# Second mixer of a two-block kernel: index heads and top-k among the projections, late attention heads in pairs, one chunk's weight residue on GpSimd

## The chip, the cores and the metric

One NeuronCore of a Trainium2 chip. The metric is the device time of one execution of the whole kernel in microseconds (us). A core has five engines that run their own instruction lists in order and wait for each other on semaphores: TensorE (PE, matmuls into PSUM; PEld is its weight load), VectorE (DVE), ScalarE (ACT), GpSimd (POOL) and SyncE (SP, which issues DMAs here).

## The reference, cut to what matters

Two blocks run one after the other on 256 tokens of width 1024. The first (three attention branches) and the expert layer at the end are untouched. Between them stands the second block's mixer:

```python
h = rms_norm_2(x, norm1_g) * (1 + scale1) + shift1
proj = h @ w_in                       # 3656 columns
xc, bg, cg, q, k, v, qi, ki, wi = jnp.split(proj, cuts, axis=-1)
conv_out = bg * short_conv(cg * xc, conv_w)
q = apply_partial_rope(rms_norm_2(q.reshape(B, S, 8, 64), q_norm_g), positions)
k = apply_partial_rope(rms_norm_2(k.reshape(B, S, 8, 64), k_norm_g), positions)
qi = apply_partial_rope(qi.reshape(B, S, 8, 64), positions)
ki = apply_partial_rope(rms_norm_2(ki, kidx_norm_g), positions)
# dsa_attention: an index picks the 64 keys that each query sees
rel = relu(einsum('bqhd,bsd->bqhs', qi, ki))
score = einsum('bqhs,bqh->bqs', rel, wi) * IDX_SCALE     # causal, then top_k
s = einsum('bqhd,bqkhd->bhqk', q, k_selected) * 64 ** -0.5
o = einsum('bhqk,bqkhd->bqhd', softmax(s), v_selected)
mix = concatenate([conv_out, attn_out], axis=-1) @ w_out
x = x + gate1 * mix                   # then norm, router, 64 experts (top 8)
```

So q, k, v and the softmax need the selection only at the scores, and the index needs only qi, ki and wi.

## The kernel before, in words

Tokens lie on partitions in NT = 2 tiles of 128. One list, `SCHEDULE` (`make_schedule`, L151 to L225), gives the order of all steps up to the router. Every engine walks this same list and issues its own part of each step, so the order of the list is the order on each engine.

**Projections.** `proj2` takes the input columns in eight chunks (`CHUNKS2`, L73): 0 qi, 1 kiwi (ki and wi, 72 columns), 2 q2, 3 k2, 4 v2, 5 xc, 6 cg, 7 bg; each for t = 0, 1 (called the first and the second half of a chunk below). A weight chunk (2 MB, 8.0 us to land) comes into one of two ring slots by SP (L533); a slot is free when the chunk two back is fully split. fp32 products are made from two parts: ScalarE rounds the chunk to an upper half `w_hi` (L787, four pieces), VectorE subtracts it from the original to get the lower half `w_lo` (L1045, four pieces), and TensorE multiplies a_hi w_hi, a_lo w_hi and a_hi w_lo: 24 matmuls a half (L1585), or 48 of half width for the three convolution chunks xc, cg, bg (L1582). There is one pair of `w_hi`, `w_lo` buffers: a piece of the next chunk may be rounded once TensorE has used the same piece in the second half (`w_used`). `with_splits` (L117) therefore puts the four `split` steps of the next chunk between the second half's matmuls and its `drain`, the step in which ScalarE or VectorE empties the PSUM bank. Two PSUM banks (`proj_b`) alternate; `bank_free` of a half lets the half after next start.

**Drains.** qi: a copy (L1111). q2, k2, kiwi: square on ScalarE (L804), sum on VectorE (L1079), power on GpSimd (L644, L648), then scaling and gains on VectorE (L1100, L1106), whose last instruction frees the bank. v2, xc: a copy on ScalarE (L810). cg: a product into `uT` (L1130). bg: three-tap convolution and product (L1143 to L1151), about 3.7 us for one half.

**Rest of the mixer.** `angles` (L1295) makes rope's arguments on VectorE, ScalarE takes the sine (L871), `rope` (L1318) rotates 25 rows of heads (q 0 to 7, k 8 to 15, qi 16 to 23, ki 24, copied to 25). `turn2` transposes the rows to T2 (L1640, copied out by ScalarE at L866) through one PSUM bank, in four groups g (q, k, qi, ki) of two tiles. `index` (L1679, relu L877, weighted sum L1333) and `topk` (L1346, a chain of MAX8 and MATCH_REPLACE) give `selmask`. For each head n = 24 to 31: `score` (two matmuls, L1677), logits plus mask (L1242), maximum (L1257), exp (L887), `flip` (transposes L1700, copied by L898), `value` (L1724), scaling by 1/sum into O2 (L1282). The logits have two buffers. Before head i's `value` matmul TensorE waits until all earlier heads have been scaled:

```python
                    if i >= 1:

                        pe.wait_ge(S("valued"), 2 * i)
```

The order around it (L205 to L221): qi, kiwi, `angles`, q2, k2, `rope`, v2, `turn2`, eight `index`, `topk` 0, xc first half, `topk` 1, xc second half; then heads 24 to 31 by `head` (L176), which puts one conv half (cg, cg, bg, bg) into each of the first four heads and none into the last four. In head n it also places `value` n-2 before that half's drain on every engine, and `flip` n-1 after it. Last the convolution rows and the turned O2 are split (`mix_conv`, `turn_branch` 3) and `out2` multiplies them.

Of the kernel before, what the change touches and what calls it, by code (L numbers as in the profile page):

```python
# [93 lines left out]
FILL2 = [1, 1, 1, 1, 0, 0, 0, 0]  # L94
# [56 lines left out]
def make_schedule():  # L151
# [53 lines left out]
    for c in range(4):  # L205
        s.extend(("proj2", c, t) for t in range(NT))
        if c == 1:
            s.append(("angles",))
    s.append(("rope",))
    groups = [[("proj2", c, t)] for c in range(4, 8) for t in range(NT)]  # L210
    take(2)
    s.append(("turn2",))
    s.extend(("index", h) for h in range(8))
    s.append(("topk", 0))
    take(1)
    s.append(("topk", 1))
# [58 lines left out]

TURNS = []
for _it in SCHEDULE:
    if _it[0] == "turn":
        TURNS.append(_it)
    if _it[0] == "turn_branch":  # L280
        TURNS += [_it + (t,) for t in range(NT)]
    if _it[0] in ("turn_merged", "norm", "start"):
        TURNS += [_it + (t, q) for t in range(NT) for q in range(2)]
    if _it[0] == "ada_out":
        TURNS.append(_it)
    if _it[0] == "turn2":
        TURNS += [_it + (g, t) for g in range(4) for t in range(NT)]
# [18 lines left out]
def build(nc, a, out):  # L306
    ctx = ExitStack()
    with ctx:
# [31 lines left out]
        nmax = sb("neg_max", [P, 2, 2])  # L340
        den = sb("den", [P, 2, 2])
        rden = sb("rden", [P, 2, 2])
# [293 lines left out]
        def _(gp):  # L636
# [15 lines left out]
            for it in RESULTS:  # L652
# [83 lines left out]
        def _(act):  # L736
# [19 lines left out]
            for it in RESULTS:  # L756
# [104 lines left out]
                if it[0] == "turn2":  # L861
                    for g in range(4):
# [15 lines left out]
                if it[0] == "score_rest":  # L878
# [5 lines left out]
                    for t in range(NT):  # L884
                        lo, w = (0, P + sink) if t == 0 else (P + 1, 2 * P + sink)
                        v = L[:, i % 2, 0:ng, lo:lo + w]
                        act.activation(v, v, ACT.Exp, bias=nmax[:, i % 2, t:t + 1],  # L887
                                       accum_out=den[:, i % 2, t:t + 1]).then_inc(S("probs"), 1)
# [73 lines left out]
        def _(dve):  # L962
# [14 lines left out]
            for it in RESULTS:  # L977
# [62 lines left out]
                if kind0 == "split":  # L1040
# [180 lines left out]
                if kind0 in ("score", "score_rest"):  # L1221
# [4 lines left out]
                    buf = L[:, i % 2]  # L1226
# [18 lines left out]
                if kind0 == "score_rest":  # L1245
# [9 lines left out]
                    for t in range(NT):  # L1255
                        lo, w = (0, P + sink) if t == 0 else (P + 1, 2 * P + sink)
                        dve.tensor_reduce(nmax[:, i % 2, t:t + 1], buf[:, 0:ng, lo:lo + w],  # L1257
                                          AX.XY, ALU.max, negate=True).then_inc(S("maxed"), 1)
                if kind0 == "flip":
# [4 lines left out]
                    dve.reciprocal(rden[:, i % 2, :], den[:, i % 2, :]).then_inc(S("rden_ready"), 1)  # L1264
                if kind0 == "value":
# [3 lines left out]
                    for t in range(NT):  # L1269
                        dve.wait_ge(S("value_product"), 2 * i + 2)  # L1270
                        ps = value_b[:, 128 * (i % 2) + 64 * t:128 * (i % 2) + 64 * t + 64]
                        if n < 24:
# [5 lines left out]
                            dve.scalar_tensor_tensor(out=o, in0=ps, scalar=rden[:, i % 2, t:t + 1], in1=o,  # L1278
                                                     op0=ALU.mult, op1=ALU.mult).then_inc(S("valued"), 1)
                        else:  # L1280
                            o = O2[:, t, HD * (n - 24):HD * (n - 24) + HD]
                            dve.tensor_scalar(o, ps, rden[:, i % 2, t:t + 1], None, ALU.mult).then_inc(S("valued"), 1)  # L1282
                if kind0 in ("angles", "rope"):
                    step = S(kind0 + "_step")
                    k = 0
# [32 lines left out]
                if kind0 == "rope":  # L1318
                    dve.wait_ge(S("trig_ready"), 1)

                    bank_taken(dve, USE["proj2", 3, 1])
                    for t in range(NT):
                        lo, hi = R[:, t, 0:25, 0:8], R[:, t, 0:25, 8:16]
                        cos = trig[:, t, 0:1, :].to_broadcast([P, 25, 8])
                        sin = trig[:, t, 1:2, :].to_broadcast([P, 25, 8])
                        for b, (src, f) in enumerate(((lo, cos), (hi, sin), (hi, cos), (lo, sin))):
                            chain(dve.tensor_tensor(rt[:, b], src, f, ALU.mult))
                        chain(dve.tensor_tensor(lo, rt[:, 0], rt[:, 1], ALU.subtract))
                        chain(dve.tensor_tensor(hi, rt[:, 2], rt[:, 3], ALU.add))
                        dve.tensor_copy(R[:, t, 25, :], R[:, t, 24, :]).then_inc(S("rows_ready"), 1)  # L1330
# [183 lines left out]
        def _(pe):  # L1514
# [18 lines left out]
            for it in SCHEDULE:  # L1533
# [99 lines left out]
                if kind0 == "turn2":  # L1633
                    pe.wait_ge(S("rows_ready"), NT)
                    for g in range(4):
# [20 lines left out]
                if kind0 in ("score", "score_rest"):  # L1656
                    n = it[1]
                    ng = len(units_of(n)) if n < 24 else 1
                    for g in range(0 if kind0 == "score" else 2, min(2, ng) if kind0 == "score" else ng):
# [10 lines left out]
                        else:  # L1670
# [20 lines left out]
                if kind0 == "flip":  # L1691
                    n = it[1]
                    i = HEADS.index(n)
                    for g in range(len(units_of(n)) if n < 24 else 1):
# [4 lines left out]
                        for b, lo in enumerate((0, P + 1, 2 * P + 1)):  # L1699
                            mm = pe.transpose(flip_b[u % 2][:, b * P:(b + 1) * P], L[:, i % 2, g, lo:lo + P], ident)  # L1700
# [240 lines left out]
```

## Time and profile before

| | |
|---|---|
| time, median of 3 runs (lowest, highest) | 1218.96 us (1215.31, 1219.78) |
| the profiled execution: own time, span in the trace | 1215.82 us, 1214.0 us |
| PE busy, share of span | 1066.8 us, 88% |
| DVE busy | 800.2 us, 66% |
| ACT busy | 569.8 us, 47% |
| POOL busy | 185.1 us, 15% |
| mean granted TensorE clock | 0.903 |
| first mixer and first norm | to 557.7 us |
| second mixer up to `out2` | 557.7 to 719.6 us |
| `out2`, norm, router, experts | 719.6 to 1214.0 us |
| load of a 2 MB chunk (`ring`), issue to landing | 8.0 us |

The profile is of one execution. A timeline row gives the start in us from the start of the span, the time, the engine, the line in the kernel, the operation and its operands; xN means N instructions merged into one row, and the bracket says how long the engine stood idle before and what released it. The end of a matmul is modelled, and neighbouring matmuls overlap. A granted clock of 1.00 is 2.4 GHz, 0.50 is 1.2 GHz.

### The profile page before, as it was taken

What the parts mean: (1) busy time and instruction counts of PE and PEld (TensorE: products, weight loads), DVE (VectorE), ACT (ScalarE), POOL (GpSimd) and SP (SyncE); (2) the same over time, 40 slices, a digit from 0 to 9 for tenths busy, and PEclk for the clock granted to TensorE, in tenths of its full rate; (3) what the DMA queues carried; (4) which work ended last, traced back from release to release, by engine and by line L of the source; (5) the groups of instructions that cost most, each with busy time, mean ns of one, the idle gap of its engine ahead of it and who ended that gap; (6) DMA issues with size and microseconds to landing.
All of it is one profiled execution on the core that took longest, in us unless ns stands there. A gap on an engine that the chain in (4) does not pass through costs nothing.

```text
span 1214.0 us, 15757 instructions
## 1 busy us (share of the span) xinstructions
PE 1066.8 (88%) x4992; PEld 852.4 (70%) x4992; DVE 800.2 (66%) x1328; ACT 569.8 (47%) x857; POOL 185.1 (15%) x231
## 2 busy tenths in 40 slices
PE   4998779967999898987978787969999999999995
PEld 3776568756766766566748666758888888888883
DVE  4556566766544644445757735368899898989995
ACT  4454333423233223233432422157777777777773
POOL 3122110010000000001200000022322323232330
PEclk9999789975899798997978857879999999999997
DMA  8452638765242823333432301378888888888882
GB/s 283 170 202 76 224 132 297 267 199 194 103 122 83 303 75 119 132 140 120 168 139 70 139 1 35 135 293 296 326 317 316 335 296 346 305 334 317 322 327 101
DMA packets 89247, 247.67 MB, mean 204 GB/s; under 512 B 11292, under 2 KB 21973, under 8 KB 75762
## 3 DMA queue, kind: packets, MB, share of 16 engines
q1 hardware_dynamic: 82914, 226.71, 51.5%
q0 software_dynamic: 6000, 19.96, 4.5%
q8 instruction: 27, 0.44, 0.1%
q10 hardware_dynamic: 288, 0.40, 0.1%
q14 instruction: 18, 0.15, 0.0%
HBM read 244.38 MB, written 2.68 MB: 204 GB/s over the span
## 4 chain that ended last, share of the span: by engine, by line
PE 41%; DVE 7%; DMA 3%; issue 2%; ACT 1%; POOL 1%; POOLq 0%; DVEq 0%; ACTq 0%
PE bank L1834 14%; PE bank L1861 7%; PE bank L1819 5%; PE bank L1585 4%; DMA x_gathered<-h_rows,block_tokens 3%; PE bank L1811 3%; DVE w_lo L1045 2%; PE bank L1582 1%; PE bank L1739 1%; PE bank L1801 1%; POOL rstd L648 1%; PE bank L1849 1%; PE bank L1731 1%; DVE score L1365 1%; PE bank L1746 1%
## 5 line engine op out<-in xcount | busy, mean ns | idle before, releaser
L1585 PE MATMUL bank<-w_hi,a_hi 128*128 128x512 f32 (+2 forms) x512 | 213.1, 416 | 24.3 <-DVE w_lo L1045 14.0
L1585 PE MATMUL bank<-w_lo,a_hi 128*128 128x512 f32 (+2 forms) x512 | 206.3, 403 | 0.0
L1585 PE MATMUL bank<-w_hi,a_lo 128*128 128x512 f32 (+2 forms) x512 | 205.6, 402 | 0.0
L1045 DVE TENSOR_TENSOR w_lo<-ring,w_hi 128x1024 fp32r<-128x1024 f32 (+2 forms) x140 | 160.1, 1180 | 61.0 <-ACT w_hi L787 57.2
L787 ACT ACTIVATE w_hi<-ring 128x1024 fp32r<-128x1024 f32 (+2 forms) x140 | 138.8, 1022 | 100.8 <-PE bank L1585 75.2
L1462 DVE TENSOR_TENSOR up_lo<-raw_weights,up_hi 128x1024 fp32r<-128x1024 f32 x136 | 163.0, 1239 | 0.0
L1585 PEld LDWEIGHTS bank<-w_hi,a_hi 128*128 128x128 f32 x512 | 103.6, 202 | 54.1 <-issue 30.7
L921 ACT ACTIVATE up_hi<-raw_weights 128x1024 fp32r<-128x1024 f32 x136 | 136.3, 1054 | 5.3 <-DMA raw_weights<-in_w_dram 5.3
L1585 PEld LDWEIGHTS bank<-w_hi,a_lo 128*128 128x128 f32 x512 | 103.4, 202 | 21.5
L1585 PEld LDWEIGHTS bank<-w_lo,a_hi 128*128 128x128 f32 x512 | 104.1, 203 | 19.8 <-issue 0.5
L644 POOL TENSOR_SCALAR mean_squares<-mean_squares 128x8 f32<-128x8 f32 (+2 forms) x32 | 6.3, 196 | 681.9 <-ACT logits L742 401.6
L887 ACT ACTIVATE logits<-logits,neg_max 128x128 f32<-128x128 f32 (+2 forms) x64 | 33.7, 528 | 159.0 <-DVE neg_max L1257 159.0
L1834 PE MATMUL bank<-up_hi,x_block_hi 128*128 128x512 f32 x264 | 105.3, 399 | 0.6 <-issue 0.6
L1834 PE MATMUL bank<-up_hi,x_block_lo 128*128 128x512 f32 x264 | 105.3, 399 | 0.0
L1834 PE MATMUL bank<-up_lo,x_block_hi 128*128 128x512 f32 x264 | 105.0, 398 | 0.0
L1481 DVE TENSOR_TENSOR down_lo<-raw_weights,down_hi 128x1024 fp32r<-128x1024 f32 x66 | 77.9, 1222 | 7.1 <-ACT down_hi L938 7.0
L731 POOL TENSOR_SCALAR put<-block_rows,consts 128x256 fp32r<-128x256 f32 x33 | 30.6, 928 | 258.5 <-PE bank L1819 130.8
L938 ACT ACTIVATE down_hi<-raw_weights 128x1024 fp32r<-128x1024 f32 x66 | 66.0, 1051 | 0.5 <-issue 0.5
L1201 DVE SCALAR_TENSOR_TENSOR ada_acc<-ring,c_col,ada_acc 128x512 f32<-128x512 f32 x84 | 63.0, 750 | 2.4
L1819 PE MATMUL bank<-y_hi,put 128*128 128x512 f32 x132 | 58.7, 445 | 6.1 <-issue 6.1
L957 ACT ACTIVATE y_hi<-bank,block_gates 128x512 fp32r<-128x512 f32 x66 | 45.5, 690 | 38.4 <-PE bank L1861 38.4
L1834 PEld LDWEIGHTS bank<-up_hi,x_block_hi 128*128 128x128 f32 x264 | 50.2, 190 | 12.8 <-issue 1.0
(250 smaller groups left out, 1890.5 us busy)
## 6 DMA issues: line engine op xcount, KB each, us to landing
raw_weights<-in_w_dram SPq DMA_DIRECT2D x102, 1024.0 KB, 6.9
ring<-in_w_in_dram SPq DMA_DIRECT2D x29, 2048.0 KB, 8.0
ring<-in_w_ada_dram SPq DMA_DIRECT2D x12, 2048.0 KB, 9.0
ring<-in_w_out_dram SPq DMA_DIRECT2D x4, 2048.0 KB, 7.9
ring<-in_w_branch_dram SPq DMA_DIRECT2D x3, 2048.0 KB, 12.5
bias<-rel_rows SPq DMA_DIRECT2D x40, 128.0 KB, 8.2
block_rows<-place_rows SPq DMA_DIRECT2D x34, 128.0 KB, 8.9
ring<-in_ws_dram SPq DMA_DIRECT2D x3, 1024.0 KB, 4.9
```

The lines of the kernel that those rows point to most:

```text
L787: act.activation(w_parts[0][:, 2 * p:2 * p + 2, 0:w], view(j, kind)[:, 2 * p:2 * p + 2, :], ACT.Copy)\
L921: act.activation(up_hi[:, r % 2, 4 * kh:4 * kh + 4, m, :], raw_up(raw[:, 1 - r % 2, :], kh, m), ACT.Copy)\
L938: act.activation(down_hi[:, f, :], raw[:, 1 - r % 2][:, UP + f * DM:UP + (f + 1) * DM], ACT.Copy)\
L957: act.activation(y_hi[:, hf * CH:(hf + 1) * CH], y_b[hf][:, :], ACT.Copy, scale=gcol[:, r, 0:1])\
L1045: dve.tensor_tensor(w_parts[1][:, 2 * p:2 * p + 2, 0:w], view(JOB[it[1:3]], kind)[:, 2 * p:2 * p + 2, :], w_parts[0][:, 2 * p:2 * p + 2, 0 ...
L1201: dve.scalar_tensor_tensor(out=o, in0=w[:, k], scalar=c_col[:, 1, k:k + 1], in1=o, op0=ALU.mult, op1=ALU.add)\
L1462: dve.tensor_tensor(up_lo[:, r % 2, 4 * kh:4 * kh + 4, m, :], raw_up(raw[:, 1 - r % 2, :], kh, m), up_hi[:, r % 2, 4 * kh:4 * kh + 4, m, : ...
L1481: dve.tensor_tensor(down_lo[:, f, :], raw[:, 1 - r % 2][:, UP + f * DM:UP + (f + 1) * DM], down_hi[:, f, :].bitcast(F32), ALU.subtract).th ...
L1585: mm = pe.matmul(ps[:, 0:w], a_parts[za][:, k, t * P:(t + 1) * P], w_parts[zw][:, k, 0:w], start=start, stop=stop)
L1819: mm = pe.matmul(acc_b[2 * t + hf][:, :], put[:, t * P:(t + 1) * P], part[:, hf * CH:hf * CH + CH], start=False, stop=False, skip_group_ch ...
L1834: mm = pe.matmul(hidden_b[:, :], (xe_hi, xe_lo)[zx][:, k, :], (up_hi, up_lo)[zw][:, r % 2, k].rearrange("p m n -> p (m n)"), start=(k == 0 ...
L1861: mm = pe.matmul(y_b[hf][:, :], (h_hi, h_lo)[zh][:, f, :], (down_hi, down_lo)[zw][:, f, hf * CH:hf * CH + CH], start=(n == 0), stop=(n == ...
```

## The change

The schedule of the second mixer is written anew; the computation is the same. The index rows (qi, ki) are roped and turned on their own ahead of k2, the index heads stand around k2's first half, both `topk` follow k2's second half, and rope and turns of q and k come later, the turns behind v2 and xc. The lower halves of xc's weights are made by GpSimd. The late heads go in pairs, with four logits buffers in the space of the two old ones and four slots for maxima and sums; the pair's scores, the flips of the pair before, one conv half, and the values of the pair before. Each rope waits for the banks of the two halves that it needs.

```diff
-FILL2 = [1, 1, 1, 1, 0, 0, 0, 0]
+POOL_SPLIT = ("w_in_2", 5)
...
     s.append(("norm", 0))
-    for c in range(4):
-        s.extend(("proj2", c, t) for t in range(NT))
-        if c == 1:
-            s.append(("angles",))
-    s.append(("rope",))
-    groups = [[("proj2", c, t)] for c in range(4, 8) for t in range(NT)]
+    groups = [[("proj2", c, t)] for c in range(8) for t in range(NT)]
     take(2)
-    s.append(("turn2",))
-    s.extend(("index", h) for h in range(8))
-    s.append(("topk", 0))
+    s.append(("angles",))
+    take(2)
+    s.append(("rope", 0))
+    take(2)
+    s.append(("turn2", 0))
+    s.extend(("index", h) for h in range(4))
     take(1)
-    s.append(("topk", 1))
+    s.extend(("index", h) for h in range(4, 8))
     take(1)
-    for h in range(8):
-        head(24 + h, FILL2[h])
-    s.append(("mix_conv",))
-    s += [("flip", 31), ("value", 30), ("value", 31), ("turn_branch", 3)]
+    s.extend(("topk", t) for t in range(NT))
+    s.append(("rope", 1))
+    take(4)
+    s.append(("turn2", 1))
+    for n in range(24, 32, 2):
+
+        s += [("score", n), ("score", n + 1), ("score_rest", n), ("score_rest", n + 1)]
+        if n > 24:
+            s += [("flip", n - 2), ("flip", n - 1)]
+        take(1)
+        if n > 24:
+            s += [("value", n - 2), ("value", n - 1)]
+    s += [("flip", 30), ("flip", 31), ("value", 30), ("value", 31), ("mix_conv",), ("turn_branch", 3)]
...
+ROPE_ROWS = ((16, 25), (0, 16))
+TURNED_ROWS = ((2, 3), (0, 1))
...
-        nmax = sb("neg_max", [P, 2, 2])
+        nmax = sb("neg_max", [P, 4, 2])
...
+        def logits_of(n):
+
+            h = n - 24
+            return L[:, n % 2] if n < 24 else L[:, h % 2, h // 2 % 2:h // 2 % 2 + 1]
...
+                if it[0] == "split" and it[1:3] == POOL_SPLIT:
+                    _, name, arg, p = it
+                    kind, w = split_kind(name, arg)
+                    gp.wait_ge(S("w_hi"), PIECES * SPLITS.index(POOL_SPLIT) + p + 1)
+                    gp.tensor_tensor(w_parts[1][:, 2 * p:2 * p + 2, 0:w], view(JOB[POOL_SPLIT], kind)[:, 2 * p:2 * p + 2, :],
+                                     w_parts[0][:, 2 * p:2 * p + 2, 0:w].bitcast(F32), ALU.subtract)\
+                      .then_inc(S("w_lo"), 1)
...
-                if kind0 == "split":
+                if kind0 == "split" and it[1:3] != POOL_SPLIT:
...
-                            dve.wait_ge(S("flipped"), UNIT[HEADS[i - 2], 0] + (len(units_of(HEADS[i - 2])) if HEADS[i - 2] < 24 else 1))
+                            prior = HEADS[i - 2] if n < 24 else max(23, n - 4)
+                            dve.wait_ge(S("flipped"), UNIT[prior, 0] + (len(units_of(prior)) if prior < 24 else 1))
...
-                    bank_taken(dve, USE["proj2", 3, 1])
...
+                    for t in range(NT):
+                        bank_taken(dve, USE["proj2", (1, 3)[it[1]], t])
...
-                    pe.wait_ge(S("rows_ready"), NT)
-                    for g in range(4):
+                    pe.wait_ge(S("rows_ready"), NT * (it[1] + 1))
+                    for g in TURNED_ROWS[it[1]]:
...
+                                pe.wait_ge(S("turn_free"), TURN["turn2", 1, 1, 1] + 1)
...
-                        pe.wait_ge(S("turn_free"), TURN["turn2", 3, 1] + 1)
+                        pe.wait_ge(S("turn_free"), TURN["turn2", 0, 3, 1] + 1)
```

The lines left out put `TURNED_ROWS` and `logits_of` into the loops of ScalarE and TensorE, and index the maxima and sums by i % 4.

## Rows read from the trace of the kernel before

**Rows 1.** Stages of the second mixer (core 0: us, then PE, PEld, DVE, ACT, POOL busy, PEclk, DMA share, GB/s)

```profile
576.90:591.65 14.75, 13.86 (x48) 10.88 (x49) 10.34 (x29) 7.48 (x10) 2.59 (x4) 0.80 0.54 195
...
611.68:628.85 17.17, 11.31 (x51) 7.97 (x51) 9.24 (x18) 8.76 (x13) 0.00 (x0) 0.85 0.54 194
...
688.30:719.56 31.26, 19.07 (x72) 14.61 (x72) 16.90 (x52) 9.54 (x31) 0.00 (x0) 0.56 0.18 67
...
sum 185.42, PE 157.05 PEld 130.04 DVE 106.95 ACT 64.21 POOL 9.61; mean PE 17.45 PEld 14.45 DVE 11.88 ACT 7.13 POOL 1.07
```

**Rows 2.** TensorE's timeline: chunk starts, the first index pair, one score, head 30's values

```profile
576.88 0.77 PE L1585 MATMUL bank<-w_hi,a_hi 128*128 128x512 f32 x1 [0.40 <-DVE w_lo L1045]
...
628.85 0.80 PE L1689 MATMUL bank<-T 64*128 64x128 f32 x4 [0.37 <-ACT T L866]
629.43 1.07 PE L1690 MATMUL bank<-T 64*128 64x256 f32 x4
...
656.19 0.55 PE L1582 MATMUL bank<-a_hi,w_hi 128*128 128x256 f32 x1 [4.68 <-DVE w_lo L1045]
...
680.46 0.39 PE L1582 MATMUL bank<-a_hi,w_hi 128*128 128x256 f32 x1
...
697.87 0.79 PE L1677 MATMUL bank<-T 64*128 64x128 f32 x2
698.46 1.06 PE L1678 MATMUL bank<-T 64*128 64x256 f32 x2
...
710.03 1.38 PE L1724 MATMUL bank<-V,probsT 128*128 128x64 f32 x6
```

**Rows 3.** VectorE's timeline (start us, us, engine line op out<-in xcount [idle before <-releaser])

```profile
571.58 0.68 DVE L1111 COPY rows<-bank 128x512 f32<-128x512 f32 x1
...
581.69 0.16 DVE L1296 CAST pos<-pos_i 128x2 f32<-128x2 int32 x1
...
585.26 0.18 DVE L1316 TENSOR_SCALAR ang<-ang 128x32 f32<-128x32 f32 x1
586.22 0.69 DVE L1079 TENSOR_REDUCE mean_squares<-squares 128x8 f32<-128x512 f32 x1 [0.78 <-ACT squares L804]
...
589.68 0.69 DVE L1106 TENSOR_TENSOR rows<-rows,g 128x512 f32<-128x512 f32 x1
590.29 4.62 DVE L1045 TENSOR_TENSOR w_lo<-ring,w_hi 128x1024 fp32r<-128x1024 f32 x4
...
611.73 1.57 DVE L1327 TENSOR_TENSOR rope_tmp<-rows,trig 128x200 f32<-128x200 f32 x4
...
639.17 0.29 DVE L1360 SCALAR_TENSOR_TENSOR score<-score,consts 128x128 f32<-128x128 f32 x1
...
654.48 0.42 DVE L1368 TENSOR_TENSOR selmask<-score,consts 128x256 f32<-128x256 f32 x1
...
693.37 0.42 DVE L1151 TENSOR_TENSOR convT<-bank,cv 128x256 f32<-128x256 f32 x1
```

**Rows 4.** ScalarE's timeline

```profile
573.60 0.22 ACT L804 ACTIVATE squares<-bank 128x64 f32<-128x64 f32 x1 [2.28 <-PE bank L1585]
...
620.24 0.60 ACT L866 ACTIVATE T<-bank 128x512 f32<-128x512 f32 x1 [0.75 <-PE bank L1640]
...
684.42 3.90 ACT L787 ACTIVATE w_hi<-ring 128x1024 fp32r<-128x1024 f32 x4
```

**Rows 5.** The granted clock in two short stretches (columns as in rows 1)

```profile
576.50:582.00 5.50, 5.12 (x12) 4.08 (x13) 4.48 (x10) 3.12 (x4) 0.74 (x2) 0.50 0.53 183
...
618.00:623.00 5.00, 1.97 (x12) 1.26 (x12) 3.38 (x3) 2.76 (x6) 0.00 (x0) 1.00 0.07 9
```

**Rows 6.** GpSimd's groups by form, whole span (line engine op names shapes xcount | busy us, mean ns | idle before)

```profile
L700 POOL TENSOR_SCALAR pick<-consts,block_cols 128x128 f32<-128x128 f32 x70 | 45.7, 658 | 33.7 <-issue 32.7
...
L648 POOL TENSOR_TENSOR rstd<-mean_squares,half_neg 128x8 f32<-128x8 f32 x22 | 36.1, 1641 | 1.8
L731 POOL TENSOR_SCALAR put<-block_rows,consts 128x256 fp32r<-128x256 f32 x33 | 30.6, 928 | 258.5 <-PE bank L1819 130.8 <-issue 127.7
```

More of the change, by code:

```diff
@@ L286 @@
     if _it[0] == "turn2":
-        TURNS += [_it + (g, t) for g in range(4) for t in range(NT)]
+        TURNS += [_it + (g, t) for g in TURNED_ROWS[_it[1]] for t in range(NT)]
 TURN = {it: n for n, it in enumerate(TURNS)}
@@ L339, in build @@
         rstd = sb("rstd", [P, 8])
-        nmax = sb("neg_max", [P, 2, 2])
-        den = sb("den", [P, 2, 2])
-        rden = sb("rden", [P, 2, 2])
+        nmax = sb("neg_max", [P, 4, 2])
+        den = sb("den", [P, 4, 2])
+        rden = sb("rden", [P, 4, 2])
         qn = sb("qn", [P, 2, CH])
@@ L885, in _ @@
                         lo, w = (0, P + sink) if t == 0 else (P + 1, 2 * P + sink)
-                        v = L[:, i % 2, 0:ng, lo:lo + w]
-                        act.activation(v, v, ACT.Exp, bias=nmax[:, i % 2, t:t + 1],
-                                       accum_out=den[:, i % 2, t:t + 1]).then_inc(S("probs"), 1)
+                        v = logits_of(n)[:, 0:ng, lo:lo + w]
+                        act.activation(v, v, ACT.Exp, bias=nmax[:, i % 4, t:t + 1],
+                                       accum_out=den[:, i % 4, t:t + 1]).then_inc(S("probs"), 1)
                 if it[0] == "flip":
@@ L1225, in _ @@
                     sink = 1 if 16 <= n < 24 else 0
-                    buf = L[:, i % 2]
+                    buf = logits_of(n)
                     for g in range(0 if kind0 == "score" else 2, min(2, ng) if kind0 == "score" else ng):
@@ L1256, in _ @@
                         lo, w = (0, P + sink) if t == 0 else (P + 1, 2 * P + sink)
-                        dve.tensor_reduce(nmax[:, i % 2, t:t + 1], buf[:, 0:ng, lo:lo + w],
+                        dve.tensor_reduce(nmax[:, i % 4, t:t + 1], buf[:, 0:ng, lo:lo + w],
                                           AX.XY, ALU.max, negate=True).then_inc(S("maxed"), 1)
@@ L1263, in _ @@
                         dve.wait_ge(S("valued"), 2 * i - 2)
-                    dve.reciprocal(rden[:, i % 2, :], den[:, i % 2, :]).then_inc(S("rden_ready"), 1)
+                    dve.reciprocal(rden[:, i % 4, :], den[:, i % 4, :]).then_inc(S("rden_ready"), 1)
                 if kind0 == "value":
@@ L1277, in _ @@
                                 bank_taken(dve, USE["proj", c, 1])
-                            dve.scalar_tensor_tensor(out=o, in0=ps, scalar=rden[:, i % 2, t:t + 1], in1=o,
+                            dve.scalar_tensor_tensor(out=o, in0=ps, scalar=rden[:, i % 4, t:t + 1], in1=o,
                                                      op0=ALU.mult, op1=ALU.mult).then_inc(S("valued"), 1)
@@ L1281, in _ @@
                             o = O2[:, t, HD * (n - 24):HD * (n - 24) + HD]
-                            dve.tensor_scalar(o, ps, rden[:, i % 2, t:t + 1], None, ALU.mult).then_inc(S("valued"), 1)
+                            dve.tensor_scalar(o, ps, rden[:, i % 4, t:t + 1], None, ALU.mult).then_inc(S("valued"), 1)
                 if kind0 in ("angles", "rope"):
                     step = S(kind0 + "_step")
-                    k = 0
+                    k = 6 * NT if it == ("rope", 1) else 0
                     def chain(ins):
@@ L1319, in _ @@
                     dve.wait_ge(S("trig_ready"), 1)
-                    bank_taken(dve, USE["proj2", 3, 1])
+                    r0, r1 = ROPE_ROWS[it[1]]
+                    nr = r1 - r0
                     for t in range(NT):
-                        lo, hi = R[:, t, 0:25, 0:8], R[:, t, 0:25, 8:16]
-                        cos = trig[:, t, 0:1, :].to_broadcast([P, 25, 8])
-                        sin = trig[:, t, 1:2, :].to_broadcast([P, 25, 8])
-                        for b, (src, f) in enumerate(((lo, cos), (hi, sin), (hi, cos), (lo, sin))):
[L1327 to L1330, printed above, removed]
+                        bank_taken(dve, USE["proj2", (1, 3)[it[1]], t])
+                    for t in range(NT):
+                        lo, hi = R[:, t, r0:r1, 0:8], R[:, t, r0:r1, 8:16]
+                        cos = trig[:, t, 0:1, :].to_broadcast([P, nr, 8])
+                        sin = trig[:, t, 1:2, :].to_broadcast([P, nr, 8])
+                        for b, (src, f) in enumerate(((lo, cos), (hi, sin), (hi, cos), (lo, sin))):
+                            chain(dve.tensor_tensor(rt[:, b, 0:nr], src, f, ALU.mult))
+                        chain(dve.tensor_tensor(lo, rt[:, 0, 0:nr], rt[:, 1, 0:nr], ALU.subtract))
+                        last = dve.tensor_tensor(hi, rt[:, 2, 0:nr], rt[:, 3, 0:nr], ALU.add)
+                        if it[1] == 0:
+                            chain(last)
+                            last = dve.tensor_copy(R[:, t, 25, :], R[:, t, 24, :])
+                        last.then_inc(S("rows_ready"), 1)
                 if kind0 == "index":
@@ L1633, in _ @@
                 if kind0 == "turn2":
-                    pe.wait_ge(S("rows_ready"), NT)
-                    for g in range(4):
+                    pe.wait_ge(S("rows_ready"), NT * (it[1] + 1))
+                    for g in TURNED_ROWS[it[1]]:
                         for t in range(NT):
@@ L1699, in _ @@
                         for b, lo in enumerate((0, P + 1, 2 * P + 1)):
-                            mm = pe.transpose(flip_b[u % 2][:, b * P:(b + 1) * P], L[:, i % 2, g, lo:lo + P], ident)
+                            mm = pe.transpose(flip_b[u % 2][:, b * P:(b + 1) * P], logits_of(n)[:, g, lo:lo + P], ident)
                         mm.then_inc(S("flipped"), 1)
```

## The prediction

> **What bounds the kernel now.** I read the stages first, then each engine's own timeline inside them. The change lies between the end of the first mixer (557.7 us) and the start of out2 (719.6 us). After that the order is untouched: out2 runs nearly closed up, then comes a serial routing chain and the expert stage, whose weight loads start only once the routing list is ready. So what the second mixer gains or loses should reach the end one for one, and I do the sum to one point: the start of out2, at 719.56.
>
> The stages [rows 1] show TensorE close to full while it has projections (13.86 of 14.75 us) and thin in three places: the turns to heads' layout (11.31 of 17.17, half of that projection), the wait for top-k and what follows it (4.68 us idle before 656.19 [rows 2]), and the last heads (19.07 of 31.26, at a mean clock of 0.56). No engine is the bound of the whole stretch, out2 included: VectorE has 107 of 185 us. The limit is hand-overs between in-order engines. VectorE's list [rows 3] holds the long pieces: the angles 3.75 us, a full norm from its sum to the gains 4.15, four lower halves of weights 4.62, a rope of 25 rows 2.5 per token tile (four products in 1.57, and two more steps and a copy), top-k 639.17 to 654.90, 15.7 in all. ScalarE [rows 4] shows a turn group's copy of 0.60 after 0.75 of waiting for its transposes, so one group each 1.34 us, and that the four upper halves of a chunk take 3.90. They can begin some 4 us into the second half of the chunk before: bg's second half began at 680.46 [rows 2], out2's first upper half at 684.42.
>
> **The change, part by part**, on the clock of the profiled run, each engine taken in its own order.
>
> *Angles ahead of kiwi's norm.* VectorE leaves qi at 572.3 and does the angles until 576.0; before, they lay beside q2's projection [rows 3]. On ScalarE the sine stands ahead of kiwi's square, at 573.60 before [rows 4] and at 576.2 now, so kiwi's first norm and q2's lower halves behind it come 2.6 us later, and q2 starts at 579.5 for 576.88 [rows 2]. TensorE is at 1.2 GHz from before q2 [rows 5] and, with as long at it as before, needs 13.9 us for q2 (the stage of 576.90 [rows 1]): end at 593.4. Cover gone: +2.6.
>
> *Rope in two parts.* 9 rows at 0.26 us x 6 + 0.1 per tile, 3.4 us on VectorE, beside q2's first half; then 16 rows, 3.9 us. Together they cost VectorE 2.2 us more than the one rope did (5.0); both lie beside TensorE's work, and uncovered they would cost that.
>
> *Turns and index between projections.* Turns of qi and kiwi: two groups of four transposes and two of one, after k2's upper halves and square on ScalarE: 593.4 to 598.4. Index heads 0 to 3: neighbours sit in different halves of the rows, and the eight matmuls of the first two heads end in 1.65 us [rows 2], so they overlap; TensorE is free at 602.1. k2's first half: 4.3 us at 1.2 GHz, then full clock, 609.7. Heads 4 to 7: TensorE 612.5, but VectorE is in k2's norm until 614.55, and ScalarE stands behind it at head 6 until 615.3, with v2's upper halves queued behind that (first ready at 613.9, made from 616.4). v2's lower halves, paced by these, end at 622.1, k2's second norm at 626.25.
>
> *Top-k under projections, xc's lower halves on GpSimd.* Top-k now runs 626.3 to 642.0, rope 1 to 645.9. TensorE has v2 (619 to 624.1; its second half waits for the bank of k2's norm: 626.3 to 631.7) and then xc, whose four lower halves GpSimd makes. No such instruction is in the trace. From below: VectorE's own, 1.16 us [rows 3], at which the upper halves would set the pace. From GpSimd's rows: one input, 128x128 at 0.66 us and 128x256 at 0.93, thus 2.1 ns an element, 2.6 us at 1024 [rows 6]; twice that for two inputs, 5.1 us, is the other end. I take 2.6, since it is the nearest row by engine. First upper half at 629.1, last lower half at 639.6. xc's first half ends at 645.2 (the clock is down until about 644), the second at 651.2.
>
> The Trainium skill (GPSIMD Engine Reference, 3.1 Elementwise) measures a two-input add of 2048 fp32 at 4497 ns on GpSimd and 2293 on VectorE; VectorE's row here, 1.16 us at 1024, agrees with the latter. By it the piece would be an estimated 2.25 us and the sum 1.4 us less.
>
> *Turns of q2 and k2, first scores.* TensorE 651.2, but ScalarE has cg's upper halves and xc's copy first (653.7); four groups of 1.34 us end at 658.3. Then the score pair, overlapped as the index heads are, at 1.2 GHz until 660.0 (one head alone takes 1.65 [rows 2]). cg's first half starts at 660.0, before at 656.19 [rows 2]. At this point the new order is 3.8 us behind.
>
> *Heads in pairs.* Per pair: scores 0.95 us at full clock, the flips of the pair before 0.9, a conv half 6.02, then the values. A head's value product waits on TensorE until every earlier head has been scaled out of its bank by VectorE. That scaling now stands behind the weight halves and the drain of the half just multiplied. Before, a head had a pass of its own and this wait lay under the next conv half. cg: first half 667.3, second 669.15 to 675.2; VectorE reaches head 24 at 679.45, so TensorE gets head 25 only at 680.0 (idle 4.0). bg: first half 682.6 to 688.65, convolution to 692.4, head 27 at 692.95 (idle 3.5). Second half 695.6 to 701.6; from its start to VectorE's last product of the convolution took 13.3 us before (680.46 to 693.79 [rows 2, 3]), so VectorE is free at 708.9 and head 29 starts at 709.45 (idle 7), the clock down again.
>
> *Tail.* Head 29 at 1.2 GHz to 710.95, the last two flips to 712.5, head 30 at 712.35. Before, head 30 began at 710.03 [rows 2], 9.53 us ahead of out2, by the same steps; the split of the convolution's rows on VectorE moves behind head 31, beside the transposes. So out2 starts at 721.9, +2.3; with 0.2 for ScalarE's square ahead of the first turns, +2.5.
>
> *Edits at nothing.* Four places for logits and for the maxima only take waits away; the weight loads stay hidden, since each slot comes free 16 us or more ahead of its next use (k2's: free at 571.7, used at 589) and a load lands in 8.0 us (the table above). "Normed banks held until the norm is done" changes nothing: the norm's last instruction freed the bank before as well, and rope only names its two banks.
>
> **Sum.** +3.8 to cg's start. From there to head 30 it took 53.8 us (656.19 to 710.03) and takes 52.35: the single heads after 695 are gone, and three waits of 14.5 in all have come: -1.5. With the 0.2: +2.5. Own time 1215.8 (span 1214.0 and 1.8 around it) gives 1218.3; the median shown stands 3.1 above the profiled execution, so 1221.5. GpSimd from 1.16 to 5.1 us: the low end gains at most 5.3, since rope 1 then sets the turns (645.9 for 651.2), 1216.2; the high end adds 10, 1231.5. A measurement of this kernel can tell about 0.5%, 6 us, from no change.
>
> **Rivals.**
> *Slower: GpSimd's halves.* Place: between v2 and xc, with TensorE waiting on each of the four. Price: 4 us for each us of one piece. It decides from 3.5 us a piece; at 5.1 the time is 1231.5. For it: this engine needs 1.64 us for a two-operand power of 8 columns [rows 6], and two operands may cost twice one. Against: its plain operations have a slope of 2.1 ns. Chance 0.24.
> *GpSimd and VectorE in each other's way.* While GpSimd works, VectorE's top-k stands. If every VectorE instruction stood behind a piece, top-k and rope would end some 10 us later, at 656, and the turns 4.7 after 651.2: 1226. If only those with two operands in SBUF do, two instructions (tile 0's mask, tile 1's first step) fall in the window, at most 5.2 us, inside the 5.3 of slack: no change. The Trainium skill (SBUF, "Who interferes with whom") states the latter: a VectorE instruction with two SBUF inputs and a GpSimd one that reads SBUF block each other. No run here shows it yet. Chance of the dear form 0.04.
> *Faster: the clock stays up.* I have 1.2 GHz in q2, k2, xc, the first pair with cg, and the tail: 2.5 + 2.2 + 1.6 + 2.4 + 5.5 = 14 us given back if TensorE never falls, 1207.5; 8.6 of it is needed for -6. For: it stays up through five us after 618 with 1.97 of work [rows 5]. Against: the gaps here are 3 to 7, and in the window 688 to 720 the mean was 0.56 [rows 1]. Together with shorter standing times than I give ScalarE and VectorE: 0.23.
> *Nothing moves, all reordered work being covered*: 1219, 0.03.
>
> **Numbers.** Forecast 0.46, its own range 1215 to 1227. Faster 0.23; slower 0.24 + 0.04; same 0.49. The range 1209 to 1232 reaches into both ends and leaves about 0.15 out.
>
> **What would show it.** Right: q2 starts near 579.5; top-k near 626 to 642 with xc under it; GpSimd pieces near 2.6 us, start to start; cg near 660; three waits of head 25, 27, 29 for VectorE of 3.5 to 7 us; out2 near 722. Wrong: pieces over 3.5 us; top-k's steps stretched while GpSimd works; the clock up through the last heads; out2 before 715.

## The result, and the profile after

The changed kernel takes **1223.82 us** (median of 16 runs, 1219.01 to 1230.94), the kernel before 1218.67 on the same chip (16 runs, 1215.21 to 1224.74). The ratio is **1.0043, with a 95% interval of 1.0027 to 1.0058**: 5.2 us slower, under the 0.5% named ahead, though the interval excludes 1. The profiled execution took 1224.31 us, span 1222.5. The page's busy times after, GpSimd 9 us up by its four new pieces (185.1 before), the others within 3 us:

```profile
PE 1063.9 (87%) x4992; PEld 851.9 (70%) x4992; DVE 802.1 (66%) x1336; ACT 568.1 (46%) x857; POOL 194.2 (16%) x235
```

All stages below are counted from their own start, the first matmul of the second mixer (557.68 us before, 562.03 after), for the code ahead of it is the same and yet its time differs from trace to trace: over the kernels of this study that start lies between 556.2 and 562.0. From there to out2's first matmul it took 161.88 us before and takes 166.31, thus **+4.4 us**. From out2 to the end the two traces differ by 0.3 us. The windows of the kernel after show this stage, the turns of q2 and k2 (654.17), the part from cg on (63.37 us before, from 656.19 [rows 2] to 719.56), then two of the waits for VectorE (677.62, 692.41) each with the work behind it (683.36, 697.93), bg's second half, and the tail from head 29's values on (columns as in [rows 1]):

```profile
562.03:728.34 166.31, 129.48 (x698) 109.66 (x699) 100.24 (x244) 57.99 (x107) 18.25 (x16) 0.81 0.32 114
654.17:662.85 8.68, 5.48 (x24) 3.42 (x24) 4.48 (x4) 4.72 (x7) 0.00 (x0) 0.61 0.34 113
662.85:728.34 65.49, 45.97 (x298) 42.24 (x297) 32.96 (x87) 20.71 (x52) 0.00 (x0) 0.76 0.22 82
677.62:682.58 4.96, 0.78 (x9) 0.67 (x7) 4.81 (x7) 2.00 (x3) 0.00 (x0) 1.00 0.04 4
683.36:686.15 2.79, 2.79 (x16) 2.14 (x15) 1.53 (x6) 0.00 (x0) 0.00 (x0) 0.50 0.99 385
692.41:696.72 4.31, 0.62 (x7) 0.51 (x6) 3.88 (x10) 0.00 (x0) 0.00 (x0) 1.00 0.00 0
697.93:700.72 2.79, 2.79 (x16) 2.14 (x15) 1.52 (x6) 0.00 (x0) 0.00 (x0) 0.50 0.00 0
700.72:708.07 7.35, 7.35 (x52) 7.35 (x51) 2.24 (x8) 4.67 (x13) 0.00 (x0) 0.79 0.00 1
715.92:728.34 12.42, 8.02 (x32) 6.56 (x33) 4.25 (x12) 3.21 (x6) 0.00 (x0) 0.50 0.20 82
```

In the waits the clock still stands at 1.00 with 0.6 to 0.8 us of work in four to five; in the work behind each it is at 0.50. TensorE's timeline after, against [rows 2]:

```profile
584.02 0.77 PE L1614 MATMUL bank<-w_hi,a_hi 128*128 128x512 f32 x1 [3.12 <-DVE w_lo L1066]
...
636.87 0.39 PE L1611 MATMUL bank<-a_hi,w_hi 128*128 128x256 f32 x1 [1.23 <-POOL w_lo L700]
639.19 0.58 PE L1611 MATMUL bank<-a_hi,w_hi 128*128 128x256 f32 x1 [1.34 <-POOL w_lo L700]
641.55 0.58 PE L1611 MATMUL bank<-a_hi,w_hi 128*128 128x256 f32 x1 [0.71 <-POOL w_lo L700]
...
654.17 0.66 PE L1669 MATMUL bank<-consts,rows 128*128 128x128 f32 x4 [1.16 <-DVE rows L1354]
...
657.57 1.11 PE L1669 MATMUL bank<-consts,rows 128*128 128x128 f32 x4 [0.69 <-ACT T L887]
659.37 1.11 PE L1669 MATMUL bank<-consts,rows 128*128 128x128 f32 x4 [0.69 <-ACT T L887]
...
682.58 0.85 PE L1754 MATMUL bank<-V,probsT 128*128 128x64 f32 x6 [4.18 <-DVE O L1304]
683.36 0.81 PE L1707 MATMUL bank<-T 64*128 64x128 f32 x4
683.94 1.08 PE L1708 MATMUL bank<-T 64*128 64x256 f32 x4
...
696.72 1.28 PE L1754 MATMUL bank<-V,probsT 128*128 128x64 f32 x6 [3.70 <-DVE O L1304]
...
715.92 1.52 PE L1754 MATMUL bank<-V,probsT 128*128 128x64 f32 x6 [7.24 <-DVE O L1304]
```

The bracket is the point of these lines: TensorE waits 3.12 us for q2's lower halves behind the moved angles, 1.23, 1.34 and 0.71 for the last three of GpSimd's pieces, and 4.18, 3.70 and 7.24 us for `O`, the scaling of the head before (heads 25, 27 and 29). The scores of a pair (the rows of 683.36 and 683.94, four matmuls each) end 1.66 us after they begin; before, those of a single head, half as many matmuls at the same clock of 0.50, took 1.65 (697.87 in [rows 2]). What stands ahead of that scaling on VectorE, for head 29, and what top-k looks like beside GpSimd, is in VectorE's timeline:

```profile
634.81 0.28 DVE L1394 MATCH_REPLACE8 score<-top,score 128x128 f32<-128x128 f32 x1
635.12 1.78 DVE L1396 TENSOR_SCALAR score<-score 128x128 f32<-128x128 f32 x1
636.94 2.35 DVE L1397 TENSOR_TENSOR selmask<-score,consts 128x128 f32<-128x128 f32 x1
639.32 2.46 DVE L1389 SCALAR_TENSOR_TENSOR score<-score,consts 128x256 f32<-128x256 f32 x1
641.82 0.43 DVE L1393 MAX8 top<-score 128x8 f32<-128x256 f32 x1
...
707.11 4.63 DVE L1066 TENSOR_TENSOR w_lo<-ring,w_hi 128x1024 fp32r<-128x1024 f32 x4 [5.11 <-ACT w_hi L808]
...
714.97 0.42 DVE L1172 TENSOR_TENSOR convT<-bank,cv 128x256 f32<-128x256 f32 x1
715.31 0.47 DVE L1304 TENSOR_SCALAR O<-bank,rden 128x64 f32<-128x64 f32 x2
```

and GpSimd's own line:

```profile
632.08 9.42 POOL L700 TENSOR_TENSOR w_lo<-ring,w_hi 128x1024 fp32r<-128x1024 f32 x4 [4.40 <-ACT w_hi L808]
```

Four pieces in 9.42 us are 2.36 each from start to start, so they end at about 634.4, 636.8, 639.1 and 641.5. The three VectorE instructions that take 1.78, 2.35 and 2.46 us end at 636.90, 639.29 and 641.78: each ends 0.1 to 0.3 us behind a piece.

### The profile page after: what moved, and what is told of

Its sections match the earlier page's. It is cut to its first block, busy times and chain, and to the rows that moved or that the text cites. A ratio compares the mean times of both kernels' runs of the same rounds, so it can differ in the third digit from the quotient of the medians.

```text
span 1222.5 us, 15771 instructions
## 1 busy us (share of the span) xinstructions
PE 1063.9 (87%) x4992; PEld 851.9 (70%) x4992; DVE 802.1 (66%) x1336; ACT 568.1 (46%) x857; POOL 194.2 (16%) x235
## 4 chain that ended last, share of the span: by engine, by line
PE 42%; DVE 4%; DMA 3%; issue 2%; ACT 1%; POOL 1%; POOLq 0%; DVEq 0%; ACTq 0%
PE bank L1864 14%; PE bank L1891 7%; PE bank L1849 5%; PE bank L1614 5%; DMA x_gathered<-h_rows,block_tokens 3%; PE bank L1611 3%; PE bank L1841 2%; PE bank L1769 1%; DVE w_lo L1066 1%; PE bank L1831 1%; POOL w_lo L700 1%; ACT w_hi L808 1%; PE bank L1761 1%; PE bank L1879 1%; PE bank L1776 1%
## 5 line engine op out<-in xcount | busy, mean ns | idle before, releaser
L1066 DVE TENSOR_TENSOR w_lo<-ring,w_hi 128x1024 fp32r<-128x1024 f32 (+2 forms) x136 | 155.2, 1179 | 63.5 <-ACT w_hi L808 59.7
```

The costliest lines, as they stand in the source:

```text
L1066: dve.tensor_tensor(w_parts[1][:, 2 * p:2 * p + 2, 0:w], view(JOB[it[1:3]], kind)[:, 2 * p:2 * p + 2, :], w_parts[0][:, 2 * p:2 * p + 2, 0 ...
```

## The experiments

Ten kernels ran beside these two. "Stage" is from the second mixer's first matmul to out2's; it falls into the part up to cg's first half and the part from there. Ratios are to the kernel before.

| kernel | us, median | ratio, 95% interval | stage | to cg | from cg |
|---|---|---|---|---|---|
| before | 1218.67 | | 161.88 | 98.51 | 63.37 |
| the change | 1223.82 | 1.0043 (1.0027 to 1.0058) | 166.31 | 100.82 | 65.49 |
| new front alone | 1219.54 | 1.0004 (0.9987 to 1.0021) | 163.49 | 100.82 | 62.67 |
| pairs alone | 1219.63 | 1.0010 (0.9993 to 1.0027) | 164.07 | 98.76 | 65.31 |
| change, second value bank | 1208.60 | 0.9916 (0.9891 to 0.9941) | 150.82 | 100.05 | 50.77 |
| change, angles back | 1224.06 | 1.0057 (1.0038 to 1.0075) | 165.53 | 99.12 | 66.41 |
| change, all halves on VectorE | 1233.01 | 1.0132 (1.0088 to 1.0176) | 175.77 | 110.43 | 65.34 |
| before, second value bank | 1216.68 | 0.9987 (0.9965 to 1.0008) | 161.55 | 99.09 | 62.46 |
| pairs alone, second value bank | 1207.48 | 0.9913 (0.9882 to 0.9944) | 149.81 | 97.98 | 51.83 |
| change, second bank, free tail | 1205.86 | 0.9895 (0.9856 to 0.9933) | 149.05 | 100.33 | 48.72 |
| pairs alone, second bank, free tail | 1203.37 | 0.9874 (0.9836 to 0.9912) | 148.62 | 99.09 | 49.53 |
| change, second bank, angles back | 1209.03 | 0.9921 (0.9886 to 0.9956) | 150.19 | 98.96 | 51.23 |

The kernel before is that of the first comparison; beside the others it took 1218.35 to 1218.9. Five kernels with the old order ahead of the heads reach cg after 97.98 to 99.09 us, four with the new one after 100.05 to 100.82. So the new front costs some 2 us there, and a single trace tells some 1 us, no less.

### The two halves of the change, each alone

New front: the heads go one by one again.

```diff
-    for n in range(24, 32, 2):
-        s += [("score", n), ("score", n + 1), ("score_rest", n), ("score_rest", n + 1)]
...
+    for h in range(8):
+        head(24 + h, 1 if h < 4 else 0)
+    s.append(("mix_conv",))
+    s += [("flip", 31), ("value", 30), ("value", 31), ("turn_branch", 3)]
```

> The changed kernel with its new front (angles, split rope and turns, index among k2, top-k under v2 and xc, xc's lower halves on GpSimd), but with the late heads one by one as before. Mixer stage = first matmul of proj2 to first matmul of out2; it is 161.9 us before and 166.3 in the change. Theory 1 (both halves cost about the same: the front puts cg's start some 2.3 us later, 98.5 before and 100.8 in the change after the stage's start; the pairs take 65.5 us from cg to out2 for 63.4): stage 163.5 to 165, time 1.5 to 3 us over before. Rival (the front is as good as before and the pairs cost it all): stage 161.5 to 162.5, time as before. Rival (the front costs it all): stage 166 or more.

Pairs: the order of before up to the heads, all lower halves on VectorE.

```diff
-POOL_SPLIT = ("w_in_2", 5)
+POOL_SPLIT = ("none", 0)
...
+    take(4)
+    s.append(("angles",))
+    take(4)
+    s += [("rope", 0), ("rope", 1)]
     take(2)
...
+    s += [("turn2", 0), ("turn2", 1)]
+    s.extend(("index", h) for h in range(8))
+    s.append(("topk", 0))
     take(1)
...
+    s.append(("topk", 1))
     take(1)
...
```

> The front as before (angles after kiwi, both ropes after k2, all turns, index and top-k together, xc's lower halves on VectorE), but the late heads in pairs. Theory 1: cg starts 98 to 99 us after the stage's start, as before, and the pairs add 2 us: stage 163.5 to 164.5. Rival, pairs cost it all: 166. Rival, front costs it all: 161.5 to 162.5. In each case three waits of TensorE for VectorE's scaling, about 4, 4 and 7 us, stand ahead of heads 25, 27 and 29.

Measured: stages of 163.49 (+1.6) and 164.07 (+2.2), together +3.8 of the +4.4. The front reaches cg 2.3 us late and the single heads get 0.7 back; the pairs lose 1.9 us from cg on, with the same three waits as in the changed kernel. TensorE's timeline of the kernel with pairs alone, then two windows of it, the last 1.6 us of the first wait and the work behind it:

```profile
677.28 1.51 PE L1751 MATMUL bank<-V,probsT 128*128 128x64 f32 x6 [4.18 <-DVE O L1301]
...
692.16 1.19 PE L1751 MATMUL bank<-V,probsT 128*128 128x64 f32 x6 [3.69 <-DVE O L1301]
...
709.83 1.51 PE L1751 MATMUL bank<-V,probsT 128*128 128x64 f32 x6 [7.23 <-DVE O L1301]
```

```profile
675.60:677.20 1.60, 0.00 (x0) 0.00 (x0) 1.53 (x4) 0.00 (x0) 0.00 (x0) 0.50 0.00 0
677.28:681.51 4.23, 4.23 (x20) 3.46 (x21) 1.52 (x6) 0.00 (x0) 0.00 (x0) 0.50 0.98 329
```

The wait is as long as in the changed kernel (4.18 us), but here the clock is down before it ends, and the values, scores and flips behind it take 4.23 us for 3.57.

Neither half gains, and neither costs much. In the medians each half alone is 1.2 or 1.3 us above before, half of the 5.2 of both together; the stages add up, the medians do not quite, and these runs don't settle that rest of some 3 us.

### A second bank for the values

The wait that the pairs bring is for a PSUM bank: all heads' values share one, and the kernel keeps TensorE from writing a bank until VectorE has read it. The odd late heads' values go to the bank of the turns, free by then, and head i waits for head i-2 alone. TensorE's part of the edit; VectorE reads from the same places:

```diff
...
-                        pe.wait_ge(S("valued"), 2 * i)
+                        pe.wait_ge(S("valued"), 2 * (i - 1 if n > 24 else i))
                     for t in range(NT):
-                        o = value_b[:, 128 * (i % 2) + 64 * t:128 * (i % 2) + 64 * t + 64]
+                        vb = turn_b if n >= 24 and n % 2 else value_b
+                        o = vb[:, 128 * (i % 2) + 64 * t:128 * (i % 2) + 64 * t + 64]
```

> The change with one thing removed: odd late heads put their value product into the turn bank, which is free there, so TensorE waits only until the head two back is scaled and the waits ahead of heads 25, 27 and 29 (4.2, 3.7 and 7.2 us) go. Theory 1 (these waits are what pairing costs, and they pull the clock down behind them): the stage falls by 8 to 12 us, to 154 to 158, and the time to 1212 to 1216, below the kernel before. Rival (VectorE's row of halves, drains and scalings is the bound there, so the wait only moves to the next step): under 3 us.

Measured: 1208.60 us, the stage 15.5 us shorter than in the changed kernel, more than either end expected; 0.8 of it lies ahead of cg, where nothing was changed, and 14.7 from cg on. TensorE's timeline of this kernel, then its windows:

```profile
674.53 1.45 PE L1756 MATMUL bank<-V,probsT 128*128 128x64 f32 x12
...
683.63 1.55 PE L1756 MATMUL bank<-V,probsT 128*128 128x64 f32 x12 [0.22 <-ACT probsT L919]
...
692.44 1.45 PE L1756 MATMUL bank<-V,probsT 128*128 128x64 f32 x12
...
701.96 2.79 PE L1756 MATMUL bank<-V,probsT 128*128 128x64 f32 x12 [7.41 <-DVE O L1305]
```

```profile
659.88:710.65 50.77, 39.47 (x299) 36.84 (x297) 32.48 (x87) 20.48 (x52) 0.00 (x0) 0.84 0.29 106
...
671.00:676.00 5.00, 5.00 (x45) 4.93 (x44) 2.27 (x2) 4.89 (x10) 0.00 (x0) 1.00 0.00 0
...
688.00:694.00 6.00, 6.00 (x54) 6.00 (x53) 3.03 (x11) 4.44 (x13) 0.00 (x0) 1.00 0.01 1
```

Each pair's twelve value matmuls now run as one, and of the three waits one is left, ahead of head 30. Against the same part after, 65.49 us, TensorE's idle time falls from 19.5 (65.49 - 45.97) to 11.3 (50.77 - 39.47), and its busy time by 6.5 for the same matmuls at a mean clock of 0.84 for 0.76. So of the 14.7 us some 8 are the waits and some 6.5 busy time, for which the clock that was down behind them is the cause that the windows show.

The second bank in the kernel before:

> The order of the kernel before, heads one by one, with only the odd late heads' value product moved to the turn bank and the wait relaxed to the head two back. Theory (the second bank pays only where two values stand together; in the old order a value's bank was free again long before): the stage stays within 1 us of 161.9 and the time within 2 us of the kernel before. Rival (the shared value bank was a cost before as well): the stage falls by 3 us or more.

Measured 0.9987 (0.9965 to 1.0008), stage 161.55: nothing that these runs can tell, as expected; before, TensorE had no wait for `O` up to head 31. And in the kernel with pairs alone:

> The order of the kernel before up to the index and top-k, heads in pairs, odd values in the turn bank. Theory (the front's 2.3 us and the pairs' waits are separate): cg starts 98.8 us after the stage's start as in the run with the old front, and from there 50 to 51.5 us follow as in the run of the change with two banks; stage 149 to 150.5, time 1206 to 1208. Rival (the two-bank gain needed the new front): 154 or more.

Measured 149.81, 0.9913, as expected for the stage, though cg came 0.8 us sooner than forecast and 51.83 us followed it. Bank and pairs together gain 12.1 us (161.88 to 149.81), where the bank alone gains 0.3 and the pairs alone lose 2.2. The new front costs 1.0 on top (150.82 for 149.81), as it cost 1.6 alone. Where the 12 us come from is seen from cg to out2, in the kernel before and in this one:

```profile
656.19:719.56 63.37, 51.01 (x301) 44.30 (x301) 36.52 (x90) 21.03 (x52) 0.00 (x0) 0.74 0.28 100
```

```profile
656.77:708.60 51.83, 40.47 (x297) 37.84 (x297) 35.67 (x90) 20.48 (x52) 0.00 (x0) 0.83 0.34 122
```

Against the kernel before, TensorE's idle time hardly changes (12.4 to 11.4 us): what goes is 10.5 us of busy time for the same heads. Two things in the rows make it: a higher clock (0.83 for 0.74), and the scores of two heads in the time of one. How the 10.5 us divide between them was not measured.

### The tail

The wait left is that of head 30, behind the last lower halves and the convolution on VectorE. With the scores done, heads 30 and 31 may write to the two banks of the scores (added to the second bank; TensorE's part again):

```diff
...
+                        pe.wait_ge(S("valued"), 2 * (i - 1 if n > 24 else i) if n < 30 else 48)
+                    if n >= 30:
+                        pe.wait_ge(S("logits"), len(UNITS))
...
+                        vb = score_b[n % 2] if n >= 30 else turn_b if n >= 24 and n % 2 else value_b
```

> The run with two banks, and heads 30 and 31 put their value products into the two score banks, free by then, so that the wait of 7.4 us ahead of head 30 goes too. VectorE still has the weight halves, the convolution and four scalings ahead of the last turns. Theory (that wait is on the path only by its last piece, since VectorE is late by itself): the stage falls by 1.5 to 3 us. Rival (the whole wait was on the path): by 6 to 7 us.

Measured 149.05, 1.8 less, as expected: most of the wait does not vanish but moves. TensorE's timeline of this kernel:

```profile
694.64 2.11 PE L1758 MATMUL bank<-V,probsT 128*128 128x64 f32 x12 [1.84 <-ACT probsT L919]
...
701.58 1.11 PE L1650 MATMUL bank<-consts,O 128*128 128x128 f32 x4 [4.83 <-DVE O L1305]
```

The values come early, and the turn of O waits 4.83 us for the same VectorE list; what is saved is a part of the 3.4 us that stood behind the wait (2.79 of value matmuls and 0.64 up to the turn). The same edit on the old front:

> The order of before up to the late heads (so xc's lower halves on VectorE), the heads in pairs, the second bank for the odd late heads' values, and heads 30 and 31 in the two banks of the scores. Theory (the pieces are independent, so their gains add): from the order of before with pairs and two banks (149.8 us from the first matmul of the second mixer to out2) the tail takes another 1.8, as it did in the changed kernel: 148.0, a ratio of 0.989 to 0.991 to the kernel before. Rival: ahead of the pairs and behind them the work is bound by different engines in the two fronts, and the tail's gain is lost here: 149.5 or more.

Measured 148.62 (148.0 forecast) and **1203.37 us, the fastest of all, 15.5 below before and 20.4 below the change**; the ratio of 0.9874 is just under the range forecast. From cg on it is 2.3 us shorter than without the tail (49.53 for 51.83), so the theory holds there; the 1.1 us by which it came later to cg lies in unchanged code.

### The angles

```diff
-    take(2)
+    take(4)
     s.append(("angles",))
-    take(2)
     s.append(("rope", 0))
```

> The change with the angles back behind kiwi's second norm (the first rope follows at once). Theory 1: q2 starts 19.2 us after the stage's start instead of 22.0, and 2 to 3 us of it reach out2: stage 163.5 to 164.5. Rival (a later step, the bank of k2's norm or top-k, takes it up): q2 starts earlier, but the stage stays at 165.5 to 166.5.

Measured: q2 starts 2.9 us sooner (19.11 into the stage for 21.99), k2 2.5, v2 1.8, cg 1.7, out2 0.8, and the median is that of the changed kernel. The forecast's +2.6 at q2 was right, the angles' place is some 1.7 of the 2.3 us by which the new front reaches cg late, and little of it reaches the end, as the rival had it. Part of what eats it is the clock: q2 takes 13.86 us here for 12.91 after, k2's first half 7.6 for 6.8, cg's first half 7.9 for 7.5. I asked whether the rest is lost in the pairs' waits:

> The change with the second bank for the odd late heads' values, and with the angles back behind kiwi's second norm. The angles alone moved cg's first half 1.7 us forward but the heads behind it lost 0.9 of that again. Theory (it was lost in the waits of the pairs, which fall on the clock): with the second bank those waits are short and the clock stays up, so the gain of 1.7 arrives whole: 149.1 us from the first matmul of the second mixer to out2, for 150.8 without the angles' move. Rival (the loss is scatter between executions, or sits in VectorE's queue whatever the bank): 150 or more.

Measured 150.19 (150.82 without the move): cg comes 1.1 us sooner and 0.5 is lost behind it again, with two of the waits gone. So the gain does not arrive whole, and the rival's number holds. All of the 0.5 is in cg's first half, 7.85 us for 7.4. Without the bank, the 0.9 lost behind cg was 0.35 up to head 25 and 0.66 right behind its wait (4.23 us up to bg's first half for 3.57, as with pairs alone). That second part is gone with the bank, as the theory had it; the first is not. Both are smaller than the 1 us that a single trace tells.

### All lower halves on VectorE

```diff
-POOL_SPLIT = ("w_in_2", 5)
+POOL_SPLIT = ("none", 0)
```

> The change with xc's lower halves back on VectorE, in its place of the list, so behind top-k and the second rope. Theory (GpSimd's four pieces of 2.36 us under top-k are worth it, and the three instructions of VectorE that stood still beside them, 5.6 us in all, lay under work of TensorE): top-k ends 5.6 us earlier, but xc starts only some 88 us after the stage's start instead of 73, cg at 107 to 109 instead of 100.8, the stage is 172 to 175 and the time 1230 to 1232. Rival (the blocking costs as much as GpSimd saves): the stage stays at 166 to 168.

Measured: stage 175.77, 9.5 us longer than with GpSimd, cg at 110.43 and 1233.01 us, each a little beyond the forecast. VectorE's timeline, then TensorE's, of this kernel:

```profile
630.74 0.23 DVE L1396 TENSOR_SCALAR score<-score 128x128 f32<-128x128 f32 x1
631.00 0.29 DVE L1397 TENSOR_TENSOR selmask<-score,consts 128x128 f32<-128x128 f32 x1
631.32 0.42 DVE L1389 SCALAR_TENSOR_TENSOR score<-score,consts 128x256 f32<-128x256 f32 x1
...
643.98 4.62 DVE L1066 TENSOR_TENSOR w_lo<-ring,w_hi 128x1024 fp32r<-128x1024 f32 x4
```

```profile
645.35 0.55 PE L1611 MATMUL bank<-a_hi,w_hi 128*128 128x256 f32 x1 [14.80 <-DVE w_lo L1066]
```

Xc waits 14.8 us behind top-k and rope: the new order stands on GpSimd's pieces. The three instructions take 0.94 us in all, for 6.59 beside GpSimd's pieces: blocking cost 5.65 us of VectorE, shown by taking the cause away.

## Why the prediction held, point by point

The sum was +3.8 to cg, -1.5 from there to head 30 and 0.2 behind it, +2.5 in all, 1221.5; measured were +2.3 to cg, +2.1 behind it, +4.4 in all, and 1223.82. Times below are into the stage.

- *Angles, q2.* Forecast 21.8, measured 21.99. "As long at 1.2 GHz as before, 13.9" was too long: 12.91.
- *Turns, index, k2.* K2 was forecast at 44.4 and began at 43.94, its first half ended at 50.7 for 52.0, v2 began at 59.8 for 61.3. The order of waits was right, the clock came back sooner: its mean was 0.83 over k2's first half, which took 6.8 us for the 7.6 forecast.
- *GpSimd's halves.* 2.6 us a piece was taken, 2.36 measured, nearer the estimate of 2.25 from the Trainium skill (GPSIMD Engine Reference, 3.1 Elementwise) than the slope of the one-input rows. Xc ended at 91.0 for 93.5. The slow rival (3.5 us and more) is ruled out.
- *GpSimd and VectorE in each other's way.* I had two instructions and 5.2 us at most, inside 5.3 of slack. It was three and 5.65; the third is a one-input TENSOR_SCALAR. Top-k began at 67.0, 1.6 sooner than forecast, and took 21.4 us for 15.7, so rope 1 ended at 92.1 for 88.2. The slack was just used up: the first turn of q waits 1.16 us for `rows L1354`. So one of the signs of being wrong that I had named came, top-k's steps stretched beside GpSimd, and cost TensorE at most these 1.16 us there. The Trainium skill (SBUF, "Who interferes with whom") has the third as well, which I had not carried over: a tensor_scalar in a two-port mode takes the shared pair, and who comes second is blocked for the whole instruction. The trace agrees, and MAX8 and MATCH_REPLACE8, with one input, stay at 0.29 and 0.28 us while a piece runs.
- *Turns of q2 and k2.* Forecast at 1.34 a group from [rows 4]; they start 1.7 to 1.8 apart, with the clock at 0.61 over the window of 654.17. Of the 2.5 us that xc had gained this gave 1.0 back: cg at 100.82 for 102.3.
- *Heads in pairs.* The three waits were forecast at 4.0, 3.5 and 7, for VectorE behind a drain, and came at 4.18, 3.70 and 7.24 us. **The failed term is what stands behind them.** I priced scores, flips and values at full clock behind the first two waits. Forecast from head 25 to bg's first half 2.6, measured 3.57 (682.58 to 686.15); from head 27 to bg's second half 2.65, measured 4.00; and that half with VectorE behind it, up to head 29, 13.85, measured 15.20, as it began at 1.2 GHz. These three are 3.7 us, and the part from cg to out2 came out at 65.49 for 62.1, 3.4 more.
- *Tail, edits at nothing.* Head 29 to out2 was 12.65 with ScalarE's 0.2, measured 12.42. Four logits places and the renamed bank waits show nothing.
- *Rivals.* The clock did not stay up. It does through most of cg and all of bg once the first two waits are gone (1.00 in both short windows of the kernel with two banks), which goes with some 6.5 us less of busy time: not by this change, but by the bank that it lacks. More than half of that lies behind heads 25 and 27, where I had full clock, and so not in the 14 us that I gave this rival.

So 2.5 us stood as the sum of a front forecast 1.5 too dear and pairs 3.4 too cheap. That the two errors go against each other is luck: without the first, the stage would have been forecast 3.4 us short and not 1.9. Both halves were small, and the result fell in the middle case for the reasons given, with the waits in the right places and one term mis-sized.

## What to carry to other kernels

Grouping two units of work puts more of them behind one shared PSUM bank: count the banks before the order, since here the pairs cost 2 us with one bank and gave 12 with two. Price what follows a TensorE wait of a few microseconds at the lower clock: of the 14.7 us that went with the waits, 6.5 were busy time. A moved step that wins at its own place (here 2.9 us) is read again at the end of the stage (0.8), not where it was moved.

## What was not expected of the hardware

- In the changed kernel the granted clock stayed at 1.00 through waits of 4.18 and 3.70 us with TensorE nearly idle, and was 0.50 through the 2.8 us of unbroken work behind each. It need not hold so long: with pairs alone the first wait, 4.18 us as well, had 0.50 in its last 1.6 us, and the 4.23 us of work behind it ran at 0.50. So what a wait costs in clock is read from the stretch after it, and two waits of one length can cost differently.
- VectorE's blocked instructions end with a GpSimd piece, so the cost hangs on the piece's length: the three of them, 0.94 us by themselves, took 6.59 beside pieces of 2.36 us. The pieces were not stretched in turn: they took 2.35 to 2.40 us each, and the first, beside which only MAX8, MATCH_VALUE_LOAD and MATCH_REPLACE8 ran, was no shorter than the others.
- The same code ahead of the change reached the second mixer between 556.2 and 562.0 us in the traces, a spread wider than what either half of the change moved; only times counted from the stage's start could be compared.
